# First loads of a two-layer decoder trunk: x quarters and weight units by turns, tables later, first unit's high part in halves

## The reference, cut to what matters

```python
for l in range(DEPTH):                       # 2
    h = rms_norm(x, norm1_g[l])
    proj = h @ w_in[l]                       # 1024 -> 6320 columns, split into the mixers' inputs
    ...                                      # gated MLP, latent attention, gated DeltaNet
    x = x + merged @ w_out[l]
    h2 = rms_norm(x, norm2_g[l])
    x = x + jnp.square(jax.nn.relu(h2 @ w_ff1[l])) @ w_ff2[l]
```

## Time and profile before

| | |
|---|---|
| median of 3 runs | 1757.25 us (1757.16 to 1757.51) |
| profiled execution | 1756.72 us, span 1754.8 us |
| TensorE busy | 1742.2 us, 99% |
| POOL busy | 1066.0 us, 61% |
| DVE busy | 957.4 us, 55% |
| ACT busy | 690.7 us, 39% |
| moved by DMA | 207.18 MB, mean 118 GB/s |

### The profile page before, as it was taken

How to read it: one execution, slowest core, us unless ns; L and a number is a source line. 1 busy time by engine, 2 the same in 40 slices (tenths; PEclk the granted TensorE clock), 3 DMA queues, 4 the chain that set the end, 5 groups by cost and what they waited for, 6 DMA issues and landing times.

```text
span 1754.8 us, 26298 instructions
## 1 busy us (share of the span) xinstructions
PE 1742.2 (99%) x10006; PEld 1427.0 (81%) x10006; DVE 957.4 (55%) x1565; ACT 690.7 (39%) x1241; POOL 1066.0 (61%) x572
## 2 busy tenths in 40 slices
PE   8999999999999999999999999999999999999999
PEld 7787888778888888888887888887888888888887
DVE  6796626653442455444566965366443435444445
ACT  6423316550104444444355243176411054444443
POOL 7554466246665777777864535662456657777776
PEclk9999999999999999999999999999999999999999
DMA  6222133123235666666542211321323356666655
GB/s 202 85 73 73 50 96 108 37 97 95 85 98 169 158 173 161 159 175 158 132 156 79 78 62 61 96 97 37 111 94 86 97 157 165 157 173 161 168 156 144
DMA packets 58896, 207.18 MB, mean 118 GB/s; under 512 B 6368, under 2 KB 8704, under 8 KB 58784
## 3 DMA queue, kind: packets, MB, share of 16 engines
q1 hardware_dynamic: 47520, 164.94, 29.9%
q0 software_dynamic: 9216, 33.56, 10.3%
q10 hardware_dynamic: 2048, 7.10, 1.1%
HBM read 184.61 MB, written 4.19 MB: 108 GB/s over the span
## 4 chain that ended last, share of the span: by engine, by line
PE 96%; ACT 1%; DVE 1%; DMA 0%; issue 0%; SPq 0%; DVEq 0%; ACTq 0%
PE ps L666 23%; PE ps L668 22%; PE ps L667 22%; PE ps L1265 6%; PE ps L1263 6%; PE ps L1264 6%; PE ps L1135 2%; PE ps L1144 1%; PE ps L1157 1%; PE ps L685 1%; PE ps L908 1%; PE ps L895 0%; PE ps L945 0%; PE ps L1207 0%; PE ps L931 0%; DMA xin<-x 0%
## 5 line engine op out<-in xcount | busy, mean ns | idle before, releaser
L666 PE MATMUL ps<-hHi,wHi 128*128 128x512 f32 x1360 | 552.9, 407 | 0.0
L668 PE MATMUL ps<-hHi,wLo 128*128 128x512 f32 x1360 | 530.3, 390 | 0.0
L667 PE MATMUL ps<-hLo,wHi 128*128 128x512 f32 x1360 | 529.8, 390 | 0.0
L566 POOL TENSOR_SCALAR wHi<-wraw 128x1024 fp32r<-128x1024 f32 x168 | 181.4, 1080 | 493.9 <-PE ps L668 477.6
L571 POOL TENSOR_TENSOR wLo<-wraw,wHi 128x1024 fp32r<-128x1024 f32 x168 | 415.8, 2475 | 13.9
L597 POOL TENSOR_TENSOR wLo<-w,wHi 128x1024 fp32r<-128x1024 f32 x96 | 237.2, 2487 | 133.6 <-ACT wHi L1694 133.5
L666 PEld LDWEIGHTS ps<-hHi,wHi 128*128 128x128 f32 x1360 | 255.4, 188 | 59.0 <-issue 6.9
L667 PEld LDWEIGHTS ps<-hLo,wHi 128*128 128x128 f32 x1360 | 255.7, 188 | 54.8 <-issue 3.8
L668 PEld LDWEIGHTS ps<-hHi,wLo 128*128 128x128 f32 x1360 | 255.3, 188 | 54.5
L1265 PE MATMUL ps<-wHi,fLo 128*128 128x512 f32 x448 | 174.3, 389 | 0.0
L1263 PE MATMUL ps<-wHi,fHi 128*128 128x512 f32 x448 | 174.3, 389 | 0.0
(11 more groups left out here) (337 smaller groups left out, 2673.0 us busy)
## 6 DMA issues: line engine op xcount, KB each, us to landing
wraw<-stream SPq DMA_DIRECT2D x224, 512.0 KB, 3.5
w<-stream SPq DMA_DIRECT2D x64, 512.0 KB, 4.4
w<-w POOLq DMA_DIRECT2D x32, 512.0 KB, 6.8
b<-stream SPq DMA_DIRECT2D x16, 512.0 KB, 3.5
b<-stream POOLq DMA_DIRECT2D x16, 512.0 KB, 6.0
w<-stream POOLq DMA_DIRECT2D x16, 512.0 KB, 8.0
xin<-x SPq DMA_DIRECT2D x4, 512.0 KB, 6.3
y<-x ACTq DMA_DIRECT2D x1, 2048.0 KB, 10.1
```

Source lines behind the costliest of these rows:

```text
L566: nc.gpsimd.tensor_scalar(wHi[:, slot], wraw[:, slot % RAW], 1.0, 0.0, ALU.mult, ALU.add).then_inc(unit_high, 1)
L666: mm(o, lh[lc], rh[rc], start=start, stop=False)
L667: mm(o, lh[lc], rl[rc], start=False, stop=False)
L668: return mm(o, ll[lc], rh[rc], start=False, stop=stop)
```

## The change

- SP issues x's quarter 0, unit 0, quarter 1, unit 1, quarter 2, quarter 3, and waits for quarter 2 to land before it issues the tables.
- POOL makes unit 0's high part by two instructions of 512 columns, the first counted in the new semaphore `first_half`, the second in `unit_high`. The increment of `split_begun`, for which nothing waits, is no longer made for unit 0.
- TensorE's `high_step` waits for `h_high` before its first matmul and for `h_lo` only before its second; for unit 0 and k below 4 it waits for the first half alone. The order of turns and steps is another.
- `lanes_zero` is merged into `lanes_set`, which then counts to 2 a layer.

```diff
             for part in range(4):
                 cols = np.s_[part * 256:(part + 1) * 256]
                 sp.dma_start(xin[:, :, cols], x[:, cols].rearrange("(t p) d -> p t d", p=P)).then_inc(x_in[part], 16)
-                if part == 1:
-                    for slot in range(RAW):
-                        load_unit(slot, slot)
+                if part < RAW:
+                    load_unit(part, part)
+            sp.wait_ge(x_in[2], 16)
             sp.dma_start(cst[:, P:], constants[:, P:NCST_F32]).then_inc(tables_in, 16)
...
-            for slot in range(RAW):
-                high(slot, 1)
+            def first_high(half, done):
+
+                cols = np.s_[half * 512:(half + 1) * 512]
+                pool.wait_ge(raw_loaded[0], 16)
+                nc.gpsimd.tensor_scalar(wHi[:, 0, cols], wraw[:, 0, cols], 1.0, 0.0, ALU.mult, ALU.add).then_inc(done, 1)
+
+            first_high(0, first_half)
+            first_high(1, unit_high)
+            high(1, 1)
             for slot in range(RAW):
                 low(slot, slot)
...
                 def high_step(slot, k):
 
-                    pe.wait_ge(unit_high, slot + 1)
+                    if slot == 0 and k < KD // 2:
+                        pe.wait_ge(first_half, 1)
+                    else:
+                        pe.wait_ge(unit_high, slot + 1)
+                    pe.wait_ge(h_high, k + 1)
+                    mm(bank_of(slot), wHi[:, slot, k * P:(k + 1) * P], hHi[:, k], start=k == 0, stop=False)
                     pe.wait_ge(h_lo, k + 1)
-                    mm(bank_of(slot), wHi[:, slot, k * P:(k + 1) * P], hHi[:, k], start=k == 0, stop=False)
                     mm(bank_of(slot), wHi[:, slot, k * P:(k + 1) * P], hLo[:, k], start=False, stop=False)
...
                 if layer == 0:
-                    turn_stream(0, range(0, 4))
+                    turn_stream(0, range(0, 2))
                     high_step(0, 0)
                     high_step(0, 1)
-                    turn_stream(0, range(4, 6))
+                    turn_stream(0, range(2, 4))
+                    high_step(0, 2)
                     high_step(1, 0)
                     high_step(1, 1)
-                    high_step(0, 2)
+                    turn_stream(0, range(4, 6))
+                    high_step(1, 2)
+                    high_step(0, 3)
+                    high_step(1, 3)
                     turn_stream(0, range(6, KD))
-                    high_step(1, 2)
-                    for k in range(3, KD):
+                    for k in range(4, KD):
                         high_step(0, k)
                         high_step(1, k)
                         if k >= 4:
...
-                nc.vector.memset(xt, 0.0).then_inc(lanes_zero, 1)
-                dve.wait_ge(lanes_zero, layer * per.lanes_zero + 1)
+                nc.vector.memset(xt, 0.0).then_inc(lanes_set, 1)
+                dve.wait_ge(lanes_set, layer * per.lanes_set + 1)
                 nc.vector.memset(ps[:, 2:4].rearrange("p b n -> p (b n)")[:, ::33], 1.0).then_inc(lanes_set, 1)
...
-                dve.wait_ge(lanes_set, layer * per.lanes_set + 1)
+                dve.wait_ge(lanes_set, layer * per.lanes_set + 2)
```

More of the change, by code:

```diff
@@ L181 @@
     qk_bcast = 8; qk_exp = 8; kqe_done = 8
-    lanes_in = 1; lanes_zero = 1; lanes_set = 1; inv_step = 62; inv_placed = 3
+    lanes_in = 1; lanes_set = 2; inv_step = 62; inv_placed = 3
     lower_done = 4; lower_copied = 4; corner_done = 4; corner_placed = 5
@@ L322, in hybrid_trunk @@
         unit_high = sem("unit_high")
-        split_begun = sem("split_begun")
+        split_begun, first_half = sem("split_begun"), sem("first_half")
         unit_split, unit_done = sem("unit_split"), sem("unit_done")
@@ L344, in hybrid_trunk @@
         qk_bcast, qk_exp, kqe_done = sem("qk_bcast"), sem("qk_exp"), sem("kqe_done")
-        lanes_in, lanes_zero, lanes_set = sem("lanes_in"), sem("lanes_zero"), sem("lanes_set")
+        lanes_in, lanes_set = sem("lanes_in"), sem("lanes_set")
         inv_step, inv_placed = sem("inv_step"), sem("inv_placed")
```

## The result

| | before | after |
|---|---|---|
| median of 22 runs each | 1757.18 us | 1759.39 us (1758.56 to 1760.57) |
| ratio | | 1.0013, 95% interval 1.0007 to 1.0018 |
| profiled execution: time, span | 1756.72, 1754.8 us | 1758.86, 1756.9 us |

The change makes the kernel 2.2 us slower: clear of the noise, and within the 0.2% that counts as no change here. The forecast was 1758.1, with a range of 1756.5 to 1760.0. The profiled span grew by 2.1 us, so the difference can be looked for in the trace.

What follows compares the result with a forecast made beforehand. TensorE, 99% busy, bounds the kernel, so only the head's delay counts. New order +0.85 us, all other terms 0, on 1757.25 gives 1758.1 us; range 1756.5 to 1760.0, with 0.95 for no change within 0.2%.

Steps and rivals of the forecast that it cites:

- the rivals: Other outcomes: low pace lasts, +1.3 to +3.3 (0.18); unit 2 late, +1 to +3.5 with other costs (0.10); gain (0.18).
- the likeliest case: TensorE's head gets slower by +0.85 us, +0.4 to +1.3, at chance 0.50.
- its own sign: Prediction wrong if transposes of blocks 2 and 3 go 0.21 apart, TensorE awaits unit 2, or squares' sum precedes 20.3.
- Tables held, cost 0, cover 1 us: SP's later table issues: POOL begins unit 2 at 20.2, ready at 23.7, before TensorE wants it at 23.93; gain 0.
- Tables, DVE's work takes 3.1 us and ends at 23.3, cost 0: DVE's work waiting for the tables, there by 20.2, ends before its next work at 25.05.
- TensorE's new order at full pace: Head with transposes of blocks 2 and 3 from 8.99 at full pace: step (0,4) at 15.63, +0.85 taken.
- Low pace until 8.99, then full: TensorE's first transposes and matmuls run at 1.2 GHz, everything from 8.99 at 2.4 GHz.
- the first rival: TensorE's low pace lasts beyond 8.99: to 12.4 +1.6 in all, to 15.8 +3.3; chance 0.18 for +1.3 to +3.3.
- Order of the loads: SP's queue: unit 0 and x's second quarter swap places, unit 0 landing at 6.4, that quarter at 7.9.
- Two halves, waits, merged semaphore at 0: POOL's halves made at 7.0 and 7.6; extra waits taken as 0, at most 1.8 us; merged semaphore 0.
- Cover of the squares: ACT's last square ends at 20.47, TensorE's sum of squares comes at 21.15, leaving 0.7 us.

Runs made afterwards that it cites:

- rope_late: Changed kernel with DVE's first rotation table made after the fifth convolution and the second after the seventh; 1758.58 us, against 1757.26 before.
- step_later: Changed kernel with steps (1,0) and (1,1) put ahead of step (0,2) on TensorE; 1758.57 us, against 1757.12 before.
- old_turns: Changed kernel with TensorE's old order of turns and steps, blocks 0 to 3 turned first; 1758.33 us, against 1757.26 before.
- whole_high: Changed kernel with unit 0's high part made in one piece, as before; 1759.47 us, against 1757.12 before.
- warm6: Changed kernel with six matmuls on zeros ahead of TensorE's first transpose; 1757.81 us, against 1757.26 before.
- hold_only: Kernel before with only SP's wait for x's third quarter before the tables added; 1757.69 us, against 1757.26 before.
- fill: Kernel before with halves, split wait and merged semaphore, and steps (0,0) to (0,3) behind blocks 0 to 3, (1,0) to (1,3) behind 4 and 5; 1757.06 us.
- no_hold: Changed kernel without SP's wait for x's third quarter before the tables; 1758.76 us, against 1757.26 before.
- loads_only: Kernel before with only the loads by turns, unit 0 second and x's second quarter third; 1758.36 us, against 1757.26 before.
- old_loads: Changed kernel with the old order of loads (x, x, unit 0, unit 1, x, x); 1759.97 us, against 1757.26 before.

## Why the prediction was right, and where it was not

The direction, the range and the call of no change beyond 0.2% held; the size did not: 2.2 us against 0.85. The measured 2.2 us lies inside the range that reached to the rivals, not inside the likeliest case's own (+0.4 to +1.3). By its own sign it was wrong: the transposes of blocks 2 and 3 still went 0.2 us apart, where full pace was forecast. So the time landed in the range by the rival's mechanism and a wait that was put at nothing, and not by the sum. Its steps one by one:

- *Tables held, cost 0, cover 1 us*: right on unit 2. POOL began it at 20.29, against 20.2 in the forecast, and TensorE did not wait for it. How near the two are is in part luck: with the same loads and the same hold it began at 18.89 to 20.56 in rope_late, step_later, old_turns, whole_high and warm6. No gain for x either (hold_only).
- *Tables, DVE's work takes 3.1 us and ends at 23.3, cost 0*: this step failed. The work was timed where POOL was mostly idle, and was moved beside POOL's work on units 2 and 3; there it took 8.4 us, from 18.94 to 27.35. It was also put behind the tables, at 20.2, while these were there by 18.94 and the last hLo set its start. xrow came 0.67 us later than rstdT's time allowed (5.42 against 4.75 from the sum of squares), and TensorE waited 0.48 at 54.81. rope_late shows that the rotation work made xrow late, and the table there that this lateness, less 0.16 to spare, is the wait. A sign of it stood in the earlier trace rows: `trig` took 0.95 us there, beside POOL's copy of 1.05 us; with nothing beside it, in hold_only, it takes 0.20.
- *TensorE's new order at full pace*: right, 0.83 measured by warm6 against 0.85 predicted, with the stalls at the places named (for hLo at 8.03, for block 2 at 11.4 to 12.1).
- *Low pace until 8.99, then full*: this step failed, and the first rival took its place at its own price: low to 12.4 was given +1.6 in all, and step (0,4) came +1.57. That the two agree so closely is luck. The transposes of blocks 2 and 3 started at 9.47 and not at 8.99, since the second matmul waited for hLo until 8.03 (7.70 forecast) and the restart at the low pace took 0.59 us; against that the pace was full earlier than 12.4: the matmul at 11.40 is 0.47 long, as others at the full pace behind transposes, and not 0.77 as at the low one. The term it adds to the sum is 0.74 in the profiled execution, and more in others of the same order.
- *Order of the loads*: unit 0 was there by 6.26, as taken. Not foreseen was that it pushes the gains' table back by 0.3 us, though that has another queue; DVE's first hLo came at 7.22 in place of 6.90. This lies within the 0.83.
- *Two halves, waits, merged semaphore at 0*: the halves gain nothing in this order (whole_high); no other row changed at the waits. Neither the split wait nor the merge was tried alone; the sum below leaves less than 0.1 us for them.
- *Cover of the squares*: ACT's last ended at 21.30, the sum of squares came at 21.96: 0.66 left, 0.7 forecast.

The sum as measured: 0.83 (order, with the gains' table) + 0.74 (pace) + 0.09 (the restart behind the last transposes: from the first matmul of step (0,4) to its second it is 0.31 now, 16.41 to 16.72, and was 0.23) + 0.48 (DVE) = 2.14, for a span that grew by 2.1. The first two terms are split by one profiled execution of warm6; the median span grew by 2.2.

## What to carry to other kernels

At a start, the order in which work can be ready is not the order that is cheapest: an in-order engine that turns from long work to a step waiting for its last operand gives up the cover that the long work was. A gap there cost twice here, once as a wait and, as far as these runs tell, once as a slower pace for some microseconds after it. Before a piece of work is moved at "cost 0", look at what runs on the other engines at the new place, and whether a row of the same work there is already longer than its twins.

## What the runs showed of the hardware

**TensorE's pace after gaps.** With transposes from 4.8 to 5.0 us on without a gap, the pace was full from 9 us in the three profiled executions of such a head without extra work (before, hold_only, fill: 9.33, 9.42, 8.76). With a gap of 0.4 to 1.6 us at about 7 it was still low at 10.2 to 13.6 in all eight profiled executions (changed, no_hold, loads_only, step_later, whole_high, old_loads, old_turns, rope_late), and full by 12.4 to 14.0. That the gap is what puts the rise off is borne out by these eight against three, and is not shown beyond that. loads_only comes nearest to varying it alone: TensorE's instructions and their order are those of before, and up to 8.9 us what differs is its gap of 0.82; the pace was low to 11.18. A gap at this place is not enough, either: warm6 has gaps of 0.57 and 0.34 there, with six matmuls from 1.99 on ahead of them, and was full by 9.16. The granted clock in the windows read 1.00 all the while; only the distance of the rows shows the pace: 0.43 us for 512 columns at the 1.2 GHz level, 0.23 at 2.4. The Trainium skill, "TensorE: Matmul & The Clock Gate", Part 1, has the two levels, and says that the moment of the rise differs from run to run; the traces agree, with full by 12.43 and low up to 13.60 for the same order.

**DVE beside POOL.** DVE instructions that read and write SBUF alone took as long as POOL's copy or subtraction beside them: in the changed kernel 2.42 and 2.43 us (at 21.45 and 24.92) in place of 0.2, with POOL's 2.36 and 2.40. Those that read PSUM (convd, 0.75) did not change. The Trainium skill, "SBUF — State Buffer", section "Who interferes with whom", says that GpSimd and VectorE share one pair of ports as an exclusive lock, which VectorE needs for two SBUF inputs or a two-port mode, and that whoever comes first keeps it for the whole instruction. The trace agrees as far as it goes: `trig`, begun at 24.92, 0.02 after POOL's subtraction, ends at 27.35, 0.05 after it.
